# A hybrid diffusion block on one Trainium2 core: the experts' third weight matrices asked for on ScalarE's DMA queue instead of SyncE's

## What is computed

```python
def run_block(args):
    tok, e = args
    xb = x_pad[tok]
    return (jax.nn.silu(xb @ w1[e]) * (xb @ w3[e])) @ w2[e]
```

## Time and profile before

| | us |
|---|---|
| Median of 3 runs | 2502.25 |
| Lowest and highest | 2495.03, 2509.82 |
| The profiled execution, its own time | 2497.47 |
| Its span, from the first to the last instruction | 2495.5 |
| TensorE busy | 2318.0 |
| VectorE busy | 1093.4 |
| ScalarE busy | 361.1 |

### The profile page before, as it was taken

How to read it: one execution, slowest core, us unless ns; L and a number is a source line. 1 busy time by engine, 2 the same in 40 slices (tenths; PEclk the granted TensorE clock), 3 DMA queues, 4 the chain that set the end, 5 groups by cost and what they waited for, 6 DMA issues and landing times. The chain is left out here.

```text
span 2495.5 us, 32789 instructions
## 1 busy us (share of the span) xinstructions
PE 2318.0 (93%) x13953; PEld 1017.0 (41%) x13954; DVE 1093.4 (44%) x2267; ACT 361.1 (14%) x645; POOL 298.1 (12%) x317
## 2 busy tenths in 40 slices
PE   5999999989999999999999899999999999999992
PEld 3555455454555523333333444444555323323331
DVE  1788377767845422222222353434454222222225
ACT  2210333331012200000000230000121000000002
POOL 2000000001000222122220000000002212222100
PEclk8999999999999999999999899999999999999996
DMA  9577111020130599999999521113107999999976
GB/s 314 193 258 268 34 26 26 17 110 34 68 152 34 214 353 401 397 412 413 393 411 404 193 90 51 47 37 109 51 34 282 385 403 400 402 401 405 408 321 252
DMA packets 139949, 574.22 MB, mean 230 GB/s; under 512 B 16898, under 2 KB 41782, under 8 KB 88216
## 3 DMA queue, kind: packets, MB, share of 16 engines
q1 hardware_dynamic: 119496, 526.48, 54.7%
q0 software_dynamic: 20224, 45.34, 4.9%
q10 hardware_dynamic: 80, 0.26, 0.0%
HBM read 550.74 MB, written 38.03 MB: 236 GB/s over the span
## 5 line engine op out<-in xcount | busy, mean ns | idle before, releaser
L1677 PE MATMUL ps<-arena 128*32 128x512 f32 x6144 | 683.6, 601 | 29.4 <-DMA arena<-in_ex_w_dram 29.4
L1677 PEld LDWEIGHTS ps<-arena 128*32 128x32 f32 x6144 | 201.4, 111 | 476.4 <-issue 476.4
L1701 PE MATMUL ps<-arena 128*32 128x512 f32 x3072 | 338.9, 592 | 4.0 <-DMA arena<-in_ex_w_dram 3.9
L2418 DVE TENSOR_TENSOR arena<-arena,ps 128x512 f32<-128x512 f32 x48 | 52.5, 1093 | 517.0 <-PE ps L1677 517.0
L1812 PE MATMUL ps<-arena 128*128 128x512 f32 x616 | 264.5, 592 | 0.0
L1557 PE MATMUL ps<-arena 128*128 128x512 f32 x512 | 229.4, 598 | 1.6 <-DVE arena L2212 1.6
L1701 PEld LDWEIGHTS ps<-arena 128*32 128x32 f32 x3072 | 106.8, 110 | 227.2 <-issue 227.2
L795 POOL DMA_INDIRECT arena<-normed_rows,arena x184 | 185.8, 1010 | 79.4 <-issue 55.1
L2463 DVE TENSOR_TENSOR arena<-ps,gates 128x512 f32<-128x512 f32 x96 | 61.8, 686 | 293.7 <-PE ps L1701 293.7
L1812 PEld LDWEIGHTS ps<-arena 128*128 128x128 f32 x616 | 117.0, 190 | 147.3 <-issue 147.3
L1370 PE MATMUL ps<-arena 128*128 128x512 f32 x384 | 167.3, 593 | 0.7 <-issue 0.7
(11 more groups left out here) (314 smaller groups left out, 2156.7 us busy)
## 6 DMA issues: line engine op xcount, KB each, us to landing
arena<-in_ex_w_dram SPq DMA_DIRECT2D x384, 1024.0 KB, 10.5
arena<-in_mod_w_dram SPq DMA_DIRECT2D x24, 2048.0 KB, 8.9
arena<-expert_rows SPq DMA_DIRECT2D x16, 1024.0 KB, 8.6
arena<-in_od_w_in_dram SPq DMA_DIRECT2D x12, 1024.0 KB, 5.3
arena<-in_x_dram SPq DMA_DIRECT2D x2, 4096.0 KB, 14.7
normed_rows<-arena POOLq DMA_DIRECT2D x16, 512.0 KB, 2.9
arena<-in_ev_w_in_dram SPq DMA_DIRECT2D x3, 2048.0 KB, 13.6
arena<-in_ev_w_in_dram SPq DMA_DIRECT2D x12, 512.0 KB, 4.1
```

The costliest lines, as they stand in the source:

```text
L1677: ins = nc.tensor.matmul(bank(2 + m)[c:c + n], x[:, j, c:c + n], w_slot(e % 2, m, KC, FE)[:, j], start=j == 0, stop=j == KC - 1)
L1701: ins = nc.tensor.matmul(bank(5 + half)[c:c + n], HT[:, j * P + c:j * P + c + n], w_slot(e % 2, 2, FC, D)[:, j, half * 512:(half + 1) * 51 ...
L2418: return V.tensor_tensor(HS.rearrange("t (c p) -> t p c", p=P), SL.rearrange("t (p c) -> t p c", c=FC), bank(3).rearrange("t (p c) -> t p ...
```

## The change

In each pass SP no longer asks for the last matrices. ScalarE asks for them instead, on its own DMA queue, between the SiLU and the copy of the hidden rows. It waits for the same two semaphores with the same values as SP did, and asks for the same halves into the same places. The last matrices of experts 0 and 1 of each layer are still asked for by SP ahead of the passes.

```diff
@@ moe_weights, in the loop over passes (SP)
                 for p in range(NP):
                     freed = [e + 2 for e in range(NE - 2) if last_pass(e) == p]
-                    freed_down = [e + 2 for e in range(NE - 2) if last_pass(e) == p - 1]
                     if freed:
...
-                    if freed_down:
-                        sp.wait_ge(half_mm, halves_before(l, p) + 3)
-                        for e in freed_down:
-                            weights(e, 2, (0,))
-                        sp.wait_ge(y_mm, n0 + p)
-                        for e in freed_down:
-                            weights(e, 2, (1,))
@@ experts (ScalarE)
+                def down_half(e, half):
+                    js = slice(half * 2, half * 2 + 2)
+                    act.dma_start(w_slot(e % 2, 2, FC, D)[:, js],
+                                  a["ex_w2"][l, e].rearrange("(p j) n -> p j n", p=P)[:, js])\
+                        .then_inc(w_full[e % 2][2], 16)
+
                 for p in range(NP):
                     act.wait_ge(up_mm, l * NP + p + 1)
                     nc.scalar.activation(SL, bank(2), ACT.Silu).then_inc(sl_ready, 1)
+                    freed_down = [e + 2 for e in range(NE - 2) if last_pass(e) == p - 1]
+                    if freed_down:
+                        act.wait_ge(half_mm, halves_before(l, p) + 3)
+                        for e in freed_down:
+                            down_half(e, 0)
+                        act.wait_ge(y_mm, l * NP + p)
+                        for e in freed_down:
+                            down_half(e, 1)
                     act.wait_ge(h_T, l * NP + p + 1)
                     nc.scalar.activation(HT, bank(4), ACT.Copy).then_inc(ht_ready, 1)
```

## The result

The changed kernel takes 2600.57 us (median of 4 runs, 2594.01 to 2603.11) against 2502.84 us of the kernel before in the same comparison. The ratio is 1.0379, 95% interval 1.0352 to 1.0405: 98 us slower. Forecast were 2589 us. The profiled execution has a span of 2599.6 us, 104 us over that of the kernel before.

A forecast was written before the change was run, and what follows sets the result against it. DMA volume was taken to bound the expert passes, 67.7 us per three against TensorE's 64.0. Fourteen groups x 9.4 = 132 us, less 45 us of present waits and clock, gave +87: 2589 us, 8-in-10 range 2500 to 2640.

The forecast's parts named there:

- The tight date and the overtaking: Eight 1 MB weight DMAs due 28.2 us after pass 3k+2 began; w2 on its own ring overtakes, each ring getting half.
- The sequencers at cost 0: ScalarE's added issues and waits cost 0, without cover 0.5 us times 14; SP gains nothing.
- The gate wait: TensorE's wait at the gate product of every third pass grows from 2.1 to 6.2 us, ends 5.7 and 7.0.
- the remainder: Gate wait now: 2.1 us measured against 0.8 reckoned; the difference was taken as transfers still queued from before.
- rival 3: SP's ring is served first, w2 steps aside at the gate: faster, 2478 us; chance 0.06.
- The wait at the last matrix: Pass 3k+4 waits for w2 of experts 4k+4 and 4k+5: 1.5 us a group, ends 0 and 2.7.
- the overlap with the first matrix of 4k+7: Its data share the engines from X + 22.5 (X: delayed gate product start), delaying w2 by 4.9 us at most.
- The clock: All fourteen gate products after waits run partly at the lower clock, losing 1.7 us each, ends 0 and 3.4.
- Not paid back: SP's queue runs empty after the gate wait; three passes take 73.4 us instead of 67.7, DMA share 0.92.
- Rival 2: Volume decides, the longer gate wait is paid back: 2502 to 2530 us, say 2515; chance 0.12.
- Rivals 1 and 3: The first of them: engines serve both rings in the order of asking, nothing moves, 2502 us; chance 0.12.
- Rival 4: Low clock lasts beyond the half product, or three rings share and x rows come late: above 2640 us; chance 0.08.

The follow-up runs named there:

- e1: Against the kernel before, only the last matrices of experts 4k+3 (32 of 120 transfers) are asked for by ScalarE; 2592.72 us, ratio 1.0370.
- e3: The changed kernel, with both last-matrix halves of experts 4k+3 asked for later, in pass 3k+3; 2556.20 us, ratio 1.0220 to the kernel before.
- e4: Against the kernel before, ScalarE instead of SP asks for all three matrices of experts 2 to 31, in the old order; 2496.74 us, ratio 0.9994.
- e8: As e1, but each half in two 0.5 MB transfers with rows of 2 KB; 2547.94 us, ratio 1.0224 to the kernel before.
- e5: Against the kernel before, only the first half of the last matrices of experts 4k+3 is asked for by ScalarE; 2560.74 us, ratio 1.0266.
- e2: Against the kernel before, the other 88 transfers go to ScalarE, those of experts 4k+3 stay with SP; 2549.88 us, ratio 1.0213.
- e9: The changed kernel with 15 spare TensorE products before the gate product in passes 3, 6, ..., 21; 2565.72 us, ratio 1.0274 to the kernel before.
- e10: The kernel before with 4 spare TensorE products before the gate product of every third pass; 2493.00 us, ratio 0.9978.
- e11: The changed kernel run again with no edit, against the kernel before on the same chip; 2593.01 us, ratio 1.0387.

## Why the prediction was right, point by point

**The tight date and the overtaking** (the order of service, rings 1:1): right, and shown. e1 puts the loss on the transfers named, e3 on their moment, e4 clears ScalarE and its ring, e8 and the packet counts show how the rings share. The forecast inferred it from q0 beside q1; q10 beside q1 does the same.

**The sequencers at cost 0:** right (e4). ScalarE's issues took 0.33 us (median of 120), not 0.49.

**The gate wait:** 6.2 us forecast, with 7.0 as the upper end; 8.1 measured, 7.7 in the second profile of the kernel. The mechanism held, the size did not, in two terms. What the queues moved from the first data of the group to TensorE's start at the gate product of pass 3 shows them: before from 904.5 to 929.2, after from 906.2 to 936.1.

```profile
q1 hardware_dynamic: 1262, 9.22, 91.2%
q0 software_dynamic: 345, 0.71, 8.4%
...
q1 hardware_dynamic: 1272, 9.30, 75.6%
q10 hardware_dynamic: 288, 2.10, 17.0%
q0 software_dynamic: 473, 1.00, 8.7%
```

The first term is the remainder of 2.1 - 0.8 = 1.3 us. The prediction took it for bytes "still queued from before" and let most of it go, since the queue would run emptier. But the eight SP transfers are 8.4 MB, and SP's ring moved 0.8 to 0.9 MB more in either kernel: a part of the request behind the last gate half is served before that half has landed. So the remainder has nothing to do with what was queued, and it stays. (For the same reason rival 3 had nothing to save there.) The second term is the price of two overtaking megabytes, 2 x 2.46 = 4.9 us; e5 and e1 measure 3.3 and 6.0 us for one and two. By their shares of the stretches, 24.7 us before and 29.9 after, the overtaking transfers took 17.0% of 29.9, 5.1 us. The gathers took 2.6 us instead of 2.1, 0.5 more, where the prediction left them at one figure although the stretch became longer. SP's ring took the same, 22.5 and 22.6. Together that is the 5.7 us by which the wait at this gate grew (6.0 on average). It is a count, and at one gate; no run changes the gathers alone.

**The wait at the last matrix:** 1.5 us a group forecast, 0 measured. The step that failed is the overlap with the first matrix of 4k+7. It counted up to 4.9 us of shared time, which holds only if the gathers fall ahead of X + 22.5 and half of w2 is still to come then; it said that it couldn't tell. In the trace they fall behind: ScalarE's ring had the engines alone from 950.5 to 957.5, 14.4 to 21.4 us behind the start of the gate product, and moved 2.9 of its 4.2 MB. The last packet of the 4.2 MB starts at 963.2, X + 27.1, about where the prediction had them without any sharing, and the product could start on time at 965.6. Where the gate wait is short (e2), the same overlap costs 2.5 us a group, within the forecast's 0 to 2.7.

**The clock:** 1.7 us forecast for each of fourteen waits, 2.2 measured: the fourteen gate products took 31 us more than at full clock (14 x 7.07 us) in both profiles of the kernel. Longer waits cost somewhat more than the one size seen before. Nor does the length of a wait alone decide whether the clock falls. Of the waits before, nine were of 2.04 us or longer, and two of these, 2.28 and 2.44 us, were followed by no loss. The first of the two:

```profile
1334.56 7.07 PE L1677 MATMUL ps<-arena 128*32 128x512 f32 x64 [2.28 <-DMA arena<-in_ex_w_dram]
```

With waits of 6.7 to 9.4 us all fourteen products were slower, as forecast. That the clock is a price of its own, not covered by the transfers, is shown by e9 (27 us); in the kernel before it is covered (e10).

**Not paid back:** right. 73.4 us a group were forecast and 0.92 of DMA, 75.3 and 74.5 with 0.93 and 0.94 measured. Rival 2 would have needed 67.7.

**The sum:** 6.2 + 1.5 + 1.7 = 9.4 us a group were forecast, 8.1 + 0 + 2.2 = 10.3 measured; two terms 2.4 us too small, one 1.5 too large. That they cancel in part is luck, and it makes the number (+98 us instead of +87) better than its terms. Rivals 1 and 3 fall with the packet counts: no order of asking, no first place for SP. Rival 4's prolonged clock did not come: the slowest product behind a wait lost 3.0 us, less than the 3.4 of a first half at the lower level. Of the signs named, one was off: w2's halves were to land 5 to 9 us after their request. In e11, where the landings in front of pass 3 can be read, they took 10.4 and 13.0 us, and the last gate half 23.3 instead of 16.6 (the last group below is two requests, with the landing of the later one):

```profile
L1149 ACTq DMA_DIRECT2D arena<-in_ex_w_dram x1: 334/334/334, 913.4 to 913.4; - x1
DMA to landing us min/median/max: 10.4/10.4/10.4
...
L1149 ACTq DMA_DIRECT2D arena<-in_ex_w_dram x1: 335/335/335, 916.8 to 916.8; - x1
DMA to landing us min/median/max: 13.0/13.0/13.0
...
L545 SPq DMA_DIRECT2D arena<-in_ex_w_dram x2: 328/380/433, 909.9 to 910.3; - x2
DMA to landing us min/median/max: 23.3/23.3/23.3
```

They did overtake it: asked for 3.1 and 6.5 us after it, they landed 10 and 4 us ahead of it.

## What to carry to other kernels

If transfers are asked for in the order in which they are needed, one ring kept that order here; a second ring let whatever was in it take its turn, packet for packet, ahead of older and more urgent work. So before moving a transfer to another engine's queue, look for the tightest landing date and count what could overtake it, at somewhat more than its bare transfer time (3.0 us for a megabyte here, not 2.46). Then ask whether the queue stays filled: where it does, as in the kernel before, a slower product costs nothing (e10); where it runs empty, as in the changed kernel, every wait is paid, and nearly every slow product too (e9).

## What was not expected of the hardware

- Rings share by packets and not by bytes: 177 packets of 2 KB against 176 of 8 KB (e8). The size of the rows is a way of setting a ring's share.
- The loss is not additive: 97 us (e1) and 54 us (e2) together make 98.
- With a single ring too, a transfer lands when part of what stands behind it in the ring has already been moved, 0.8 MB at the gate of pass 3.
- In one execution of the changed kernel, what waits for the end of the first product (the SiLU and SP's second request) started late in 39 of 48 passes, in the one shown by 1.7 us, while TensorE's next signals were on time. The few longer products at full clock are of this execution too. Its second profile (e11) shows none of it, and the cause stays open.
